# The last two row tiles of an output projection taken together, state sums spread between products, and one subtraction moved ahead of the weight sums

## The chip, the cores and the metric

The kernel runs on one core of a Trainium2 chip. The metric is the device time of one execution in microseconds. For the kernel before it is 1906.66 us, the median of three runs (1905.7 to 1906.89).

## What is computed

One decoder block on 2048 positions of 1024 channels, in float32:

```python
h = rmsnorm(x, norm_mix); proj = h @ w_in
c = conv4(proj[:, :512]); y_lru = rg_lru(c) * gelu(proj[:, 512:1024])
glu = proj[:, 1024:1536] * sigmoid(proj[:, 1536:])
y_cm = silu(layernorm(conv31(glu)))
x = x + concat(rmsnorm(y_lru), rmsnorm(y_cm)) @ w_out
h = rmsnorm(x, norm_ffn)
x = x + (silu(h @ w_gate) * (h @ w_up)) @ w_down
return rmsnorm(x, norm_final)
```

## The kernel before, in words

Every float32 product is made of three float32r products, high by high, high by low and low by high: an operand's high part is a rounding copy (by ScalarE as a rule), its low part is a subtraction (by GpSimd or VectorE). Four things follow one another: the input projection with both branches (to about 415 us), the output projection (415 to 624 us), the gate and up projections by a Strassen-like scheme of seven products (to about 1470 us for both halves of the positions), and the down projection.

**Output projection.** The 2048 positions are 16 row tiles, NT = 16, here called rows 0 to 15. A row has four products of 12 matmuls, one for each bank e = 0 to 3: e 0 and 1 (group 0) take the first four channel chunks (the LRU branch), e 2 and 3 (group 1) the last four. VectorE adds each bank, scaled, to the residual line (add_row, line 1729), counting s_outf[e]; TensorE's product for bank e of row w waits until the same bank of row w - 1 has been read. ScalarE splits y into y_hi (y_split, line 1260), GpSimd makes y_lo (line 888). After add_row, ScalarE takes the root of the row's mean square (row_std, lines 1351 and 1352), VectorE scales the row (row_scaled, hn, line 1903), TensorE transposes it (turn_h2, line 2312) after the next row's products, and ScalarE copies the transposed tile out (h2_copy, line 1346).

Beside rows 1 to 9 the normalisation of the two branches runs. Its sums over channels are matmuls with a vector of 1/512: norm_columns (line 2195) has one output column per matmul. For m = 1 it has no folded operand, so it makes 16 such sums, recorded as 32 matmuls, after row 1; norm_var (line 2187) comes right behind it.

**Into the gate and up projections.** For the first half the seven moving operands a[0] to a[6] are made while the last rows run: VectorE sums four of them (first_half_sum), ScalarE makes the high parts (a_high, line 1356), and GpSimd makes the low parts 0, 1 and 6 (a_low, line 938), VectorE 2, 3, 4 and 5 (a_low, line 1863). VectorE also makes the weight sums of every matrix, four instructions (weight_sum, line 1887); ScalarE and GpSimd split them (t_hi, line 1366, t_lo, line 933), and the raw weights (b_hi, b_lo, line 927). t_sum, a_hi[2] and a_hi[3] lie where the group 0 weights of the output projection were, a_hi[4] to a_hi[6] where those of group 1 were, so the first can begin when the last product of group 0 is done.

Matrix m has products n = 0 to 6, each 12 matmuls, in the order 0 (matrix m), then 1, 2, 3, 4, 5, then 0 of the next matrix, then 6. Product n of the first matrix of a half waits for low part n. Before products 4 and 5 of the first matrix TensorE also turns rows 14 and 15.

Each engine runs its instructions in the order written. The order on GpSimd at rows 14 and 15 is: y_lo of row 14, b_lo, a_lo 0, y_lo of row 15, a_lo 1. On VectorE, with row 15: bank reads of group 0, four weight sums, a_lo 2, bank reads of group 1, a_lo 3; then in the first matrix_block a sum, hn of row 14, a_lo 4, hn of row 15, a_lo 5, four weight sums of the next matrix.

The second half starts in second_half_block (VectorE): a sum of product results, a_lo 4 and 5, the four weight sums, sum12, a_lo 6, sum22. Product 6 of that matrix waits for sum22 (gt, line 1959).

Of the kernel before, what the change touches and what calls it, by code (L numbers as in the profile page):

```python
# [22 lines left out]
P = 128  # L23
TILE = 512
# [6 lines left out]
def hybrid_block(nc, x, norm_mix, w_in, conv4_w, conv4_b, gate_a_w, gate_a_b, gate_x_w, gate_x_b,  # L31
# [4 lines left out]
    NJ = CH // P  # L36
# [7 lines left out]
    NT = S // P  # L44
# [32 lines left out]
    with ExitStack() as ctx:  # L77
# [332 lines left out]
        def yb(w):  # L410

            return 4 + w if w < 2 else (w + 1) % 2 if w < TPH else 2 + w % 2

        def from_sbuf(w):

# [371 lines left out]
        def _(pool):  # L787
# [164 lines left out]
            for w in range(3, NT):  # L952
                if w > 4:
                    y_lo_part(w)
                if w == NT - 2:
                    raw_lo(0, 0)
                    pool.wait_ge(s_sum0, 4)
                    a_low(0)
                if w == NT - 1:
                    a_low(1)  # L960
                for m, first in NORM_STEP.items():
                    if w == {2: 3, 3: 6}[m]:
                        fold(m, "mean")
                    if w - first == 2:
                        for what in ("lru", "var") if m == 2 else ("var", "lru"):
                            fold(m, what)
                    if w - first == 4:
                        fold(m, "cm")
# [89 lines left out]
        def _(act):  # L1058
# [313 lines left out]
            for w in range(NT):  # L1372
                if w == 1:
                    row_std(1)
                    norm_swish(1, between=DIRECT[1], turned=0)
                    h2_copy(1)
                if 4 <= w < NT - 1:
                    y_split(w + 1)
                if w == 4:
                    norm_rms_cm(1, 5)  # L1380
                for m, first in NORM_STEP.items():
                    if w - first == 1:
                        squares_lru(m)
                        if w == 4:
                            h2_copy(2)
                            h2_copy(3)
                        squares_cm(m)
                    if w - first == 2:
                        norm_std(m, 5)
                        if m == 2:  # L1390
                            norm_rms_lru(m, 4)
                    if w - first == 3:
                        norm_swish(m)
                    if w - first == 4:
                        norm_rms_cm(m, 5)
                if w == NT - 1:
                    act.wait_ge(s_sum0, 4)
                    act.wait_ge(s_out[1], NT)
                    a_high(2)
                    sums_hi(0, 0)  # L1400
                    a_high(3)
                    row_std(w)
                if 5 <= w < NT - 1:
                    h2_copy(w - 1)
                if 1 < w < NT - 1:
                    row_std(w)
                if w - NORM_STEP[3] == 3:
                    norm_rms_lru(3, 4)
                if w == LOAD_AT + 3:
                    act.wait_ge(s_a0, 64)  # L1410
                    a_high(0)
                    a_high(1)
                    raw_hi(0, 0, 1)
# [154 lines left out]
        def _(dve):  # L1568
# [143 lines left out]
            def add_row(w, between=None, groups=(0, 1)):  # L1712

                if w == 4:
                    norm_rms(1)
                if w % 4 == 0:
                    dve.wait_ge(s_rms, w // 4 + 1)
                dve.wait_ge(s_xr[w % 4], 16 * (w // 4 + 1 + (2, 1, 1, 1)[w % 4]))
                line = row[w % 4]
                for group in groups:  # L1720
                    if group and between:
                        between()
                    for dh in range(2):
                        e = 2 * group + dh
                        cols = slice(dh * TILE, (dh + 1) * TILE)
                        dve.wait_ge(s_out[e], w + 1)
                        if group:
                            dve.wait_ge(s_outf[dh], w + 1)
                        v.scalar_tensor_tensor(out=line[:, cols], in0=ps[e],
                                               scalar=rms[:, 2 * w + group:2 * w + group + 1],  # L1730
                                               in1=line[:, cols], op0=ALU.mult, op1=ALU.add).then_inc(s_outf[e], 1)

# [156 lines left out]
            def first_weight_sums():  # L1889
                for n in range(4):  # L1890
                    weight_sum(0, 0, n, 1)
                a_low(0, 2)

            def row_scaled(w):
                dve.wait_ge(s_std2, w + 1)
# [17 lines left out]
            for w in range(NT):  # L1913
                if w == 0:
                    add_row(2)
                    row_scaled(0)
                elif w > 2:
                    add_row(w, first_weight_sums if w == NT - 1 else lambda: norm_between(w))
                if w == NT - 1:
                    a_low(0, 3)  # L1920
                if w == 3:
                    row_scaled(2)
                if w == 1 or 3 <= w < NT - 2:
                    row_scaled(w)
                for m, first in NORM_STEP.items():
                    if w - first == 4:
                        norm_rms(m)
                if w in SUM_AT:
                    for n in range(2):
                        first_half_sum(2 * SUM_AT.index(w) + n)  # L1930
# [62 lines left out]
            def matrix_block(m, i, b, h, first=False, count=None, last=False, early=(), late=(), second=False):  # L1993

                if first and not b:
# [1 line left out]
                    row_scaled(NT - 2)  # L1997
                    a_low(0, early[0])
                    row_scaled(NT - 1)
                    a_low(0, early[1])  # L2000
                    dve.wait_ge(s_hn, NT)
                    for n in range(2):
                        dve.wait_ge(s_x2st[n], 16 * NT // 2)
# [26 lines left out]
            def second_half_block(m, i, count):  # L2030

                sum11(m, i, 0, 1, True)
                a_low(1, 4)
                a_low(1, 5)
                dve.wait_ge(s_pr[6], m)
                for n in range(4):
                    weight_sum(m + 1, 1, n, count)
                sum12(m, i, 0, 1, True)
                a_low(1, 6)
                sum22(m, i, 0, 1, True)  # L2040
                hidden21(i - 1, 0)
                for n in range(2):
# [2 lines left out]
                f_sum(2, i - 1, 0)  # L2045
                f_sum2(i - 1, 0)

            matrix_block(0, 0, 0, 0, first=True, count=1, early=(4, 5))
            matrix_block(1, 0, 1, 0, first=True, count=2)
            for h in range(NH):  # L2050
                if h:
# [74 lines left out]
        def _(pe):  # L2126
# [60 lines left out]
                    mm = pe.matmul(ps[bank], mean_w[:, :], tile[:, j], start=j == 0, stop=j == chunks - 1)  # L2187
                mm.then_inc(done, 1)

            def norm_columns(m, what, bank, done):  # L2190

                tile, chunks = summed(m, what)
                for t in range(TILE // P):
                    for j in range(chunks):
                        mm = pe.matmul(ps[bank][:, t:t + 1], tile[:, j, t * P:(t + 1) * P], mean_w[:, 0:1],
                                       start=j == 0, stop=j == chunks - 1)
                mm.then_inc(done, 1)

            def norm_mean(m, bank):
                norm_rows(m, "mean", bank, s_mean)  # L2200
# [1 line left out]
            def norm_var(m, bank):  # L2202
                norm_rows(m, "var", bank, s_var)

            def norm_sums_lru(m, bank):
                norm_columns(m, "lru", bank, s_rm2)

            def norm_sums_cm(m, bank):
                norm_columns(m, "cm", bank, s_rm1)
# [131 lines left out]
                        pe.wait_ge(s_dc, m + 1)  # L2341
                        norm_sums_lru(m, 4)

            for w in range(NT):
                b = yb(w)
                pe.wait_ge(s_ylo, w + 1)
                for group in range(2):
                    if group:
                        norm_sums(w)
                    if w == 0:  # L2350
                        pe.wait_ge(s_wlo, FIRST_APART + PPAIRS + WOQ // 2 * (group + 1))
                    for dh in range(2):
                        e = 2 * group + dh
                        if e == 3:
                            norm_steps(w)
                        cols = slice(dh * TILE, (dh + 1) * TILE)
                        if w:
                            pe.wait_ge(s_outf[e], w)
                        elif e == 3:
                            gates_tile(UNITS - 1, 1)  # L2360
                            pe.wait_ge(s_dc, 2)
                        product(ps[e],
                                (lambda k: y_hi[b][:, k], lambda k: y_lo[b][:, k]),
                                (lambda k: wo_hi[:, k, cols], lambda k: wo_lo[:, k, cols]),
                                range(group * NJ, (group + 1) * NJ)).then_inc(s_out[e], 1)
                if w == 1:
                    free_aux(1, AUX_USES)
                    norm_sums_lru(1, 7)
                    free_aux(0, AUX_USES)
                    norm_var(1, 6)  # L2370
                for turned in TURNED.get(w, (w - 1,) if 5 <= w < NT - 1 else ()):
                    turn_h2(turned)


            BANKS = [[ps[4], ps[5], ps[0], ps[5], ps[0], ps[5], ps[5]], [ps[4], ps[1], ps[0], ps[1], ps[0], ps[1], ps[1]]]
# [42 lines left out]
            def last_rows(n):  # L2418

                if n in (4, 5):  # L2420
                    turn_h2(NT - 6 + n)
                if n == 2:
                    for e in range(2):
                        pe.wait_ge(s_outf[e], NT)

            pe.wait_ge(s_rsty, 4)
            pe.wait_ge(s_rsts, 4)
            matrix_product(0, 0, 0, 0, 0, first=True)
            two_matrices(0, 0, new_half=0, first=True, between=last_rows)
            for h in range(NH):  # L2430
# [64 lines left out]
```

## Time and profile before

| | |
|---|---|
| median of three runs | 1906.66 us (1905.7 to 1906.89) |
| the profiled execution | 1904.58 us |
| its span in the profile | 1902.7 us |
| TensorE busy | 1875.1 us, 99% of the span |
| VectorE, ScalarE, GpSimd busy | 1106.6, 808.4, 1144.9 us |
| mean granted TensorE clock | 0.996 |

A granted clock of 1.00 is 2.4 GHz, 0.50 is 1.2 GHz. Times of the trace count from the start of the span. Matmuls are pipelined: the start of the next tells more than the length of one. PE is TensorE, DVE is VectorE, ACT is ScalarE, POOL is GpSimd. In a row of the timeline the first number is the start, the second the length from first to last of the merged instructions, both in us.

### The profile page before, as it was taken

Reading aid. Unit: us, or ns where it says so; the run is one execution under the profiler, and the core shown is the slowest. Engines: PE = TensorE matmul, PEld = TensorE weight load, DVE = VectorE, ACT = ScalarE, POOL = GpSimd, SP = SyncE. Lnnn points to the kernel's source line nnn. Section 1 sums busy time; section 2 is a strip of 40 time slices with the busy share of each in tenths; the row PEclk is TensorE's granted clock in tenths of the full one; section 3 lists DMA queues with packets and bytes.
Section 4 is the critical chain, followed back from the end, with each engine's and each line's share of the span. In section 5 each row is a group of like instructions: output and inputs, shape, how many; then the busy total and the mean of one; then the engine's idle time right before and its main releaser. Section 6 shows DMA issues by size and latency. Waiting matters only on the chain.

```text
span 1902.7 us, 22499 instructions
## 1 busy us (share of the span) xinstructions
PE 1875.1 (99%) x8374; PEld 1544.2 (81%) x8374; DVE 1106.6 (58%) x1269; ACT 808.4 (42%) x938; POOL 1144.9 (60%) x427
## 2 busy tenths in 40 slices
PE   9999999999999999999999999999999999999998
PEld 7888788877788788888888788888888888888886
DVE  6899988997645755455545854445443025433535
ACT  6466766585643533333333433333333222232235
POOL 3577477945734465666655755555555676676663
PEclk9999999999999999999999999999999999999999
DMA  6222132265777334533355433323333765655455
GB/s 196 78 79 88 45 100 78 75 224 172 247 240 231 117 125 127 153 119 127 112 153 176 151 105 114 106 88 105 115 105 127 288 225 190 210 189 211 166 198 221
DMA packets 240946, 284.20 MB, mean 149 GB/s; under 512 B 12095, under 2 KB 166207, under 8 KB 240364
## 3 DMA queue, kind: packets, MB, share of 16 engines
q1 hardware_dynamic: 240874, 283.25, 44.8%
q8 instruction: 45, 0.74, 0.2%
q14 instruction: 25, 0.20, 0.0%
q10 hardware_dynamic: 2, 0.00, 0.0%
HBM read 200.90 MB, written 82.31 MB: 149 GB/s over the span
## 4 chain that ended last, share of the span: by engine, by line
PE 82%; POOL 6%; DVE 5%; ACT 2%; issue 2%; DMA 2%; POOLq 0%; SPq 0%; DVEq 0%; ACTq 0%
PE ps L2133 19%; PE ps L2135 19%; PE ps L2134 19%; PE acc L2133 8%; PE acc L2135 8%; PE acc L2134 8%; DVE a_lo L1863 1%; POOL nsq L877 1%; PE ps L2161 1%; DVE t_sum L1887 1%; POOL nsq L879 1%; POOL w_lo L804 1%; POOL f_lo L1018 0%; DVE wo_lo L1707 0%; POOL glu L827 0%
## 5 line engine op out<-in xcount | busy, mean ns | idle before, releaser
L933 POOL TENSOR_TENSOR t_lo<-t_sum,t_hi 128x2048 fp32r<-128x2048 f32 x44 | 205.6, 4674 | 165.3 <-ACT t_hi L1366 165.2
L927 POOL TENSOR_TENSOR b_lo<-m_raw,b_hi 128x1536 fp32r<-128x1536 f32 x44 | 157.6, 3582 | 179.2 <-ACT b_hi L1361 121.9
L1018 POOL TENSOR_TENSOR f_lo<-f_raw,f_hi 128x2048 fp32r<-128x2048 f32 (+1 forms) x42 | 182.2, 4338 | 129.3 <-ACT f_hi L1518 124.8
L2133 PE MATMUL ps<-h_hi,w_hi 128*128 128x512 f32 x512 | 201.1, 393 | 0.8 <-POOL w_lo L804 0.8
L2135 PE MATMUL ps<-h_hi,w_lo 128*128 128x512 f32 x512 | 199.4, 389 | 0.0
L2134 PE MATMUL ps<-h_lo,w_hi 128*128 128x512 f32 x512 | 199.2, 389 | 0.0
L1887 DVE TENSOR_TENSOR t_sum<-m_raw 128x512 f32<-128x512 f32 x88 | 141.7, 1630 | 97.4 <-PE acc L2135 87.6
L1518 ACT CAST f_hi<-f_raw 128x2048 fp32r<-128x2048 f32 (+1 forms) x42 | 74.3, 1769 | 263.6 <-PE ps L2135 168.1
L2133 PE MATMUL ps<-wd_hi,f_hi 128*128 128x512 f32 x462 | 179.8, 389 | 0.8 <-POOL wd_lo L1025 0.8
L2134 PE MATMUL ps<-wd_lo,f_hi 128*128 128x512 f32 x462 | 179.7, 389 | 0.0
L2135 PE MATMUL ps<-wd_hi,f_lo 128*128 128x512 f32 x462 | 179.7, 389 | 0.0
L2076 DVE TENSOR_TENSOR wd_raw<-wd_raw 128x1024 f32<-128x1024 f32 (+1 forms) x30 | 73.6, 2453 | 174.8 <-DMA wd_raw<-in_w_down 174.8
L2133 PE MATMUL ps<-a_hi,t_hi 128*128 128x512 f32 x440 | 171.5, 390 | 0.8 <-DVE p5s L1959 0.8
L2134 PE MATMUL ps<-a_lo,t_hi 128*128 128x512 f32 x440 | 171.2, 389 | 0.0
L2135 PE MATMUL ps<-a_hi,t_lo 128*128 128x512 f32 x440 | 171.2, 389 | 0.0
L2133 PEld LDWEIGHTS ps<-h_hi,w_hi 128*128 128x128 f32 x512 | 96.1, 188 | 20.8 <-POOL w_lo L804 1.2
L2135 PEld LDWEIGHTS ps<-h_hi,w_lo 128*128 128x128 f32 x512 | 96.1, 188 | 20.3
L2134 PEld LDWEIGHTS ps<-h_lo,w_hi 128*128 128x128 f32 x512 | 96.2, 188 | 19.6 <-issue 0.2
L2133 PE MATMUL acc<-a_hi,t_hi 128*128 128x512 f32 x264 | 103.7, 393 | 4.0 <-DVE gt L1959 2.4
L2133 PE MATMUL ps<-a_hi,b_hi 128*128 128x512 f32 x264 | 102.9, 390 | 4.2 <-DVE a_lo L1863 2.6
L2133 PE MATMUL ps<-wo_hi,y_hi 128*128 128x512 f32 x256 | 104.6, 409 | 2.3 <-DVE wo_lo L1707 1.0
L2134 PE MATMUL acc<-a_lo,t_hi 128*128 128x512 f32 x264 | 103.3, 391 | 0.0
(257 smaller groups left out, 4689.1 us busy)
## 6 DMA issues: line engine op xcount, KB each, us to landing
f_raw<-f_scr SPq DMA_DIRECT2D x35, 1024.0 KB, 4.9
wd_raw<-in_w_down SPq DMA_DIRECT2D x60, 512.0 KB, 6.6
f_scr<-fs SPq DMA_DIRECT2D x110, 256.0 KB, 2.1
m_raw<-in_w_gate SPq DMA_DIRECT2D x88, 256.0 KB, 3.9
m_raw<-in_w_up SPq DMA_DIRECT2D x88, 256.0 KB, 5.1
w_raw<-in_w_in SPq DMA_DIRECT2D x32, 512.0 KB, 5.3
f_scr<-gt SPq DMA_DIRECT2D x44, 256.0 KB, 2.0
xt<-in_x SPq DMA_DIRECT2D x16, 512.0 KB, 6.3
```

The costliest lines, as they stand in the source:

```text
L804: g.tensor_tensor(w_lo[q % 2][:, :, :, :], w_raw[q % 2][:, :, :, :], f32(w_hi[q % 2][:, :, :, :]), ALU.subtract).then_inc(s_wlo, 1)
L877: g.tensor_tensor(into[:, 0:2], source[:, 0:2], source[:, 2:4], ALU.add).then_inc(s_fold, 1)
L879: g.tensor_tensor(into[:, 0], into[:, 0], into[:, 1], ALU.add).then_inc(s_fold, 1)
L927: g.tensor_tensor(b_lo[b][:, :, :, :], m_raw[b][:, 0:3], f32(b_hi[b][:, :, :, :]), ALU.subtract).then_inc(s_mlo, 1)
L933: g.tensor_tensor(t_lo[b][:, :, :, :], t_sum[b][:, :, :, :], f32(t_hi[b][:, :, :, :]), ALU.subtract).then_inc(s_mlo, 1)
L1018: g.tensor_tensor(f_lo[j % 3][:, 0:n], f_raw[j % 2][:, 0:n], f32(f_hi[j % 3][:, 0:n]), ALU.subtract).then_inc(s_dlo, 1)
L1518: a.copy(f_hi[j % 3][:, 0:n], f_raw[j % 2][:, 0:n]).then_inc(s_dhi, 1)
L1887: v.tensor_tensor(into, in0, in1, ALU.subtract).then_inc(s_t, 1)
L2076: v.tensor_tensor(raw[:, 0, 0:c1 - c0], raw[:, 0, 0:c1 - c0], raw[:, 1, 0:c1 - c0], WD[m][2]).then_inc(s_t, 1)
L2133: pe.matmul(bank, lhs[0](c), rhs[0](c), start=first, stop=False, skip_group_check=more)
L2134: pe.matmul(bank, lhs[0](c), rhs[1](c), start=False, stop=False, skip_group_check=more)
L2135: mm = pe.matmul(bank, lhs[1](c), rhs[0](c), start=False, stop=last, skip_group_check=more)
```

## The change

Five edits:

1. The state sums of m = 1 are spread: after each of the four products of row 1, TensorE makes the sums of one of four groups of 128 positions (8 recorded matmuls).
2. Rows 14 and 15 are interleaved on TensorE: group 0 of row 14, group 0 of row 15 (into banks 4 and 5, out_bank), the turning of row 13, group 1 of row 14, group 1 of row 15. VectorE reads in the order row 14 group 0, row 15 group 0, the four weight sums, row 14 group 1, a_lo 2, row 15 group 1, a_lo 3, a_lo 4.
3. To have y of row 15 earlier, ScalarE's y_split(15) goes ahead of row_std(13), and GpSimd makes y_lo of row 15 right after that of row 14; b_lo, a_lo 0 and a_lo 1 follow.
4. ScalarE's a_high(2), sums_hi and a_high(3) move to row 14, around h2_copy(13) and ahead of row_std(14).
5. In the second half's first block VectorE makes a_lo 6 ahead of the weight sums.

```diff
 GpSimd
             for w in range(3, NT):
                 if w > 4:
                     y_lo_part(w)
-                if w == NT - 2:
+                if w == NT - 1:
                     raw_lo(0, 0)
                     pool.wait_ge(s_sum0, 4)
                     a_low(0)
-                if w == NT - 1:
                     a_low(1)
 ScalarE
-                if 4 <= w < NT - 1:
+                if 4 <= w < NT - 2:
                     y_split(w + 1)
...
-                if w == NT - 1:
+                if w == NT - 2:
                     act.wait_ge(s_sum0, 4)
                     act.wait_ge(s_out[1], NT)
                     a_high(2)
+                if 5 <= w < NT - 1:
+                    h2_copy(w - 1)
+                if w == NT - 3:
+                    y_split(NT - 1)
+                if w == NT - 2:
                     sums_hi(0, 0)
                     a_high(3)
-                    row_std(w)
-                if 5 <= w < NT - 1:
-                    h2_copy(w - 1)
-                if 1 < w < NT - 1:
+                if w > 1:
                     row_std(w)
 VectorE
+                elif 2 < w < NT - 2:
+                    add_row(w, lambda: norm_between(w))
+                elif w == NT - 2:
+                    add_row(NT - 2, groups=(0,))
+                    add_row(NT - 1, groups=(0,))
+                    first_weight_sums()
+                    add_row(NT - 2, groups=(1,))
+                    a_low(0, 2)
+                elif w == NT - 1:
+                    add_row(NT - 1, groups=(1,))
                     a_low(0, 3)
+                    a_low(0, 4)
...
                     row_scaled(NT - 2)
                     a_low(0, early[0])
                     row_scaled(NT - 1)
-                    a_low(0, early[1])
...
                 a_low(1, 4)
                 a_low(1, 5)
+                a_low(1, 6)
                 dve.wait_ge(s_pr[6], m)
                 for n in range(4):
                     weight_sum(m + 1, 1, n, count)
                 sum12(m, i, 0, 1, True)
-                a_low(1, 6)
                 sum22(m, i, 0, 1, True)
...
-            matrix_block(0, 0, 0, 0, first=True, count=1, early=(4, 5))
+            matrix_block(0, 0, 0, 0, first=True, count=1, early=(5,))
 TensorE
+        def out_bank(w, e):
+            return 4 + e if w == NT - 1 and e < 2 else e
...
+            def row_group(w, group):
...
+                    if w and out_bank(w, e) == e:
+                        pe.wait_ge(s_outf[e], w)
...
+                    if w == 1:
+                        free_aux(1, AUX_USES)
+                        norm_sums_lru(1, 7, (e,))
+
+            for w in range(NT - 1):
+                row_group(w, 0)
+                if w == NT - 2:
+                    row_group(NT - 1, 0)
+                    turn_h2(w - 1)
+                row_group(w, 1)
...
+            row_group(NT - 1, 1)
```

The wait of the first matrix for the reads of banks 0 and 1 of row 15 moves ahead of its product 0, and the waits for the last normalisation sums move to the start of row 15.

## Rows read from the trace of the kernel before

**Rows 1.** The page, busy time of TensorE over the span.
```profile
PE 1875.1 (99%) x8374; PEld 1544.2 (81%) x8374; DVE 1106.6 (58%) x1269; ACT 808.4 (42%) x938; POOL 1144.9 (60%) x427
```
**Rows 2.** Waits of TensorE, whole run: total us, times, longest.
```profile
PE ps L2133 <- DVE a_lo L1863: 2.6, 1, 2.6
PE acc L2133 <- DVE gt L1959: 2.4, 1, 2.4
...
PE acc L2133 <- POOL a_lo L938: 1.6, 1, 1.6
...
PE ps L2133 <- DVE row L1729: 0.6, 1, 0.6
```
**Rows 3.** Timeline of TensorE between rows 1 and 2.
```profile
439.45 3.94 PE L2195 MATMUL ps<-mean_w,ny 128*128 128x1 f32 x32
443.25 2.05 PE L2187 MATMUL ps<-nsq,mean_w 128*128 128x512 f32 x2
```
**Rows 4.** Windows: stretch, length, TensorE busy (count), granted clock, DMA share, GB/s.
```profile
442.60:449.40 6.80, 6.80 (x18) 0.50 0.11 46
...
638.70:642.20 3.50, 3.50 (x19) 1.00 0.31 93
...
1074.10:1077.50 3.40, 3.40 (x10) 0.50 0.23 67
```
**Rows 5.** Timeline of VectorE and GpSimd during row 2.
```profile
447.99 4.45 DVE L1697 TENSOR_TENSOR_SCAN cv<-uw,hl,su 128x1024 f32<-128x1024 f32 x1 [0.21 <-POOL su L869]
...
457.92 0.75 DVE L1729 SCALAR_TENSOR_TENSOR row<-ps,rms,row 128x512 f32<-128x512 f32 x1
...
447.91 2.39 POOL L888 TENSOR_TENSOR y_lo<-y_raw,y_hi 128x1024 fp32r<-128x1024 f32 x1
```
**Rows 6.** Timeline of TensorE: rows 14 and 15 begin, product 6.
```profile
601.34 0.47 PE L2133 MATMUL ps<-wo_hi,y_hi 128*128 128x512 f32 x1
...
613.14 0.48 PE L2133 MATMUL ps<-wo_hi,y_hi 128*128 128x512 f32 x1
...
649.59 0.50 PE L2133 MATMUL acc<-a_hi,t_hi 128*128 128x512 f32 x1 [1.56 <-POOL a_lo L938]
```
**Rows 7.** Timeline of ScalarE, rows 13 and 14.
```profile
601.24 1.07 ACT L1346 COPY h2t<-ps 128x512 f32<-128x512 f32 x2 [2.92 <-PE ps L2312]
...
603.60 1.04 ACT L1260 CAST y_hi<-y_raw 128x1024 fp32r<-128x1024 f32 x1
```
**Rows 8.** Timeline of GpSimd from row 14 to the first matrix.
```profile
600.75 3.50 POOL L927 TENSOR_TENSOR b_lo<-m_raw,b_hi 128x1536 fp32r<-128x1536 f32 x1
...
612.12 4.61 POOL L938 TENSOR_TENSOR a_lo<-a_raw,a_hi 128x2048 fp32r<-128x2048 f32 x1
624.32 4.67 POOL L933 TENSOR_TENSOR t_lo<-t_sum,t_hi 128x2048 fp32r<-128x2048 f32 x1 [7.59 <-ACT t_hi L1366]
```
**Rows 9.** Timeline of VectorE from row 13 to the first matrix.
```profile
603.92 1.42 DVE L1903 SCALAR_TENSOR_TENSOR hn<-row,rstd,g_row 128x1024 f32<-128x1024 f32 x1
...
619.55 1.28 DVE L1887 TENSOR_TENSOR t_sum<-m_raw 128x512 f32<-128x512 f32 x2
...
626.09 5.05 DVE L1863 TENSOR_TENSOR a_lo<-a_raw,a_hi 128x2048 fp32r<-128x2048 f32 x1 [0.28 <-ACT a_hi L1356]
...
633.05 5.57 DVE L1863 TENSOR_TENSOR a_lo<-a_raw,a_hi 128x2048 fp32r<-128x2048 f32 x1
```
**Rows 10.** Timeline of VectorE and GpSimd, start of the second half.
```profile
1057.82 6.07 DVE L1863 TENSOR_TENSOR a_lo<-a_raw,a_hi 128x2048 fp32r<-128x2048 f32 x2
1063.82 4.59 DVE L1887 TENSOR_TENSOR t_sum<-m_raw 128x512 f32<-128x512 f32 x2
...
1061.71 5.55 POOL L927 TENSOR_TENSOR b_lo<-m_raw,b_hi 128x1536 fp32r<-128x1536 f32 x1
```
**Rows 11.** Timeline of ScalarE and VectorE, a[6] of the second half.
```profile
1063.32 1.93 ACT L1356 CAST a_hi<-a_raw 128x2048 fp32r<-128x2048 f32 x1
...
1070.38 2.28 DVE L1863 TENSOR_TENSOR a_lo<-a_raw,a_hi 128x2048 fp32r<-128x2048 f32 x1
```

More of the change, by code:

```diff
@@ L1728, in add_row @@
                             dve.wait_ge(s_outf[dh], w + 1)
-                        v.scalar_tensor_tensor(out=line[:, cols], in0=ps[e],
+                        v.scalar_tensor_tensor(out=line[:, cols], in0=ps[out_bank(w, e)],
                                                scalar=rms[:, 2 * w + group:2 * w + group + 1],
@@ L1891, in first_weight_sums @@
                     weight_sum(0, 0, n, 1)
-                a_low(0, 2)
             def row_scaled(w):
@@ L1916, in _ @@
                     row_scaled(0)
-                elif w > 2:
-                    add_row(w, first_weight_sums if w == NT - 1 else lambda: norm_between(w))
-                if w == NT - 1:
+                elif 2 < w < NT - 2:
[8 more added lines that the diff above has]
+                    add_row(NT - 1, groups=(1,))
                     a_low(0, 3)
+                    a_low(0, 4)
                 if w == 3:
@@ L2188, in norm_rows, with norm_columns @@
                 mm.then_inc(done, 1)
-            def norm_columns(m, what, bank, done):
+            def norm_columns(m, what, bank, done, tiles=range(TILE // P)):
                 tile, chunks = summed(m, what)
-                for t in range(TILE // P):
+                for t in tiles:
                     for j in range(chunks):
@@ L2196, in norm_columns @@
                                        start=j == 0, stop=j == chunks - 1)
-                mm.then_inc(done, 1)
+                if t == TILE // P - 1:
+                    mm.then_inc(done, 1)
             def norm_mean(m, bank):
@@ L2203, in norm_var, with norm_sums_lru @@
                 norm_rows(m, "var", bank, s_var)
-            def norm_sums_lru(m, bank):
-                norm_columns(m, "lru", bank, s_rm2)
+            def norm_sums_lru(m, bank, tiles=range(TILE // P)):
+                norm_columns(m, "lru", bank, s_rm2, tiles)
             def norm_sums_cm(m, bank):
@@ L2342, in norm_steps @@
                         norm_sums_lru(m, 4)
-            for w in range(NT):
+            def row_group(w, group):
                 b = yb(w)
[L2346 to L2365, printed above, removed]
+                if not group:
+                    pe.wait_ge(s_ylo, w + 1)
+                    if w == NT - 1:
+                        pe.wait_ge(s_rsty, 4)
+                        pe.wait_ge(s_rsts, 4)
+                else:
+                    norm_sums(w)
+                if w == 0:
+                    pe.wait_ge(s_wlo, FIRST_APART + PPAIRS + WOQ // 2 * (group + 1))
+                for dh in range(2):
+                    e = 2 * group + dh
+                    if e == 3:
+                        norm_steps(w)
+                    cols = slice(dh * TILE, (dh + 1) * TILE)
+                    if w and out_bank(w, e) == e:
+                        pe.wait_ge(s_outf[e], w)
+                    elif e == 3:
+                        gates_tile(UNITS - 1, 1)
+                        pe.wait_ge(s_dc, 2)
+                    product(ps[out_bank(w, e)],
+                            (lambda k: y_hi[b][:, k], lambda k: y_lo[b][:, k]),
+                            (lambda k: wo_hi[:, k, cols], lambda k: wo_lo[:, k, cols]),
+                            range(group * NJ, (group + 1) * NJ)).then_inc(s_out[e], 1)
+                    if w == 1:
+                        free_aux(1, AUX_USES)
+                        norm_sums_lru(1, 7, (e,))
@@ L2366, in _ @@
+            for w in range(NT - 1):
[4 more added lines that the diff above has]
+                row_group(w, 1)
                 if w == 1:
-                    free_aux(1, AUX_USES)
-                    norm_sums_lru(1, 7)
                     free_aux(0, AUX_USES)
                     norm_var(1, 6)
-                for turned in TURNED.get(w, (w - 1,) if 5 <= w < NT - 1 else ()):
+                for turned in TURNED.get(w, (w - 1,) if 5 <= w < NT - 2 else ()):
@@ L2421, in last_rows @@
                     turn_h2(NT - 6 + n)
[L2422 to L2427, printed above, removed]
+            for e in range(2):
+                pe.wait_ge(s_outf[e], NT)
             matrix_product(0, 0, 0, 0, 0, first=True)
```

## The prediction

> **What bounds the kernel now.** I read the page first: TensorE is busy for 1875.1 of 1902.7 us [rows 1], so only its idle time and its slow clock can be won, and only where the change touches them. The waits of TensorE come next [rows 2]: in the first matrix of the first half it waits 2.6 us for a low part by VectorE (operand 4) and 1.6 us for one by GpSimd (operand 6), in the first block of the second half 2.4 us for VectorE's sum22, and ahead of row 3 it waits 0.6 us for VectorE's read of row 2. These are the four places that the edits reach. Third, the granted clock [rows 4]: it is 0.50 (1.2 GHz) for the 6.8 us from 442.6, behind the thin sums of row 1, and for the 3.4 us from 1074.1, behind the 2.4 us wait; behind the 2.6 us wait in the first half it stays at 1.00. Last, the timelines around each place, engine by engine [rows 3, 5 to 11].
>
> A product of twelve matmuls takes 2.72 us: row 15 begins 11.80 us after row 14 [rows 6], which holds 48 matmuls and a turning of 0.9 us, so 0.227 us a matmul. At the half clock it is about 0.43 us: ten matmuls touch the 3.40 us from 1074.1 [rows 4], of which the first and the last reach over its ends, so some 8 fit where 15 would.
>
> **State sums spread (edit 1).** Thirty-two thin matmuls take 3.94 us behind row 1 and norm_var starts at 443.25 [rows 3]. Spread, they take as long, 8 behind each product, so norm_var starts when it did. What should go is the half clock of [rows 4]: 13 or so products of row 2 and norm_var ran in it, and row 2 should end some 3 us earlier, near 455.0 instead of 458.0 (48 matmuls of 0.227 us from about 444.1). But row 3 then waits for VectorE's read of row 2's bank 0. It starts at 457.92 and lasts 0.75 [rows 5], and nothing in front of it depends on TensorE's rows: the scan takes 4.45 us from 447.99, since GpSimd's y_lo of 447.91 to 450.30 goes first [rows 5], then come a reciprocal and a scaling. Bank 3 of row 1 is finished 1.3 us later than VectorE asks for it (the sums of three products stand ahead of it, 2.7 us), so VectorE's convolution ends 1.3 us later; the scan would be issued at 449.3 and still get through behind the same y_lo at 450.3, so this costs nothing while that cover of 2.3 us holds. The gain is therefore 0, and TensorE's idle time ahead of row 3 grows from 0.6 to about 3.8 us. The half clock followed an idle 2.4 us and not one of 2.6 us, so behind 3.8 us I take it as likely. A stretch of 3.4 us at 0.50 loses 1.6 us (7 matmuls of 0.227 that no longer fit). Bounds: 0 and +3.2 (6.8 us of it, as in the first case); I take +1.6, from the 3.4 us case, which also followed an idle wait.
>
> **Rows 14 and 15 (edits 2 to 4).** TensorE's work is the same and it is full up to 618.7, if y_lo of row 15 is there at 606.8 (601.3 + 5.45). ScalarE makes y_hi of row 15 right behind the copy of row 12, which ends at 602.3 [rows 7], so 602.2 to 603.3; GpSimd's y_lo takes 2.4 us [rows 5], so 603.4 to 605.8. It is in time by 1 us. For this ScalarE's row_std of row 13 comes 1.04 us later, and VectorE's hn of row 13 is ready to start at 604.96 instead of 603.92 [rows 9].
>
> Now the edit's price. VectorE's two-source operations on SBUF and GpSimd's operations exclude one another, and when both wait they take turns: in [rows 10] b_lo, 3.50 us alone [rows 8], is issued at 1061.71 and takes 5.55, since it waits for VectorE's a_lo to end at 1063.9; the weight sums queued right behind that a_lo don't go first but wait until b_lo has ended at 1067.26 (two sums take 4.59 us instead of 1.28 [rows 9, 10]). Bank reads (0.75 us [rows 5]) have a PSUM source, and I take them as not held. The Trainium skill has the same in "SBUF — State Buffer", in its section on the shared port pair: an exclusive lock, held for the whole instruction by whoever starts first. It names no turn-taking; by its rule alone VectorE could run its four sums in one go, the second rival below.
>
> In order, on GpSimd: y_lo to 605.8; hn of row 13, waiting, goes next (1.15 us), to 606.95; b_lo 3.5 us to 610.4; a_lo 0, 4.6 us [rows 8], to 615.0; then a_lo 1 is queued. VectorE reads bank 1 of row 15 (product ends at 612.4, row 14 and 15 group 0 having taken 10.9 us from 601.3) by 613.3 and asks for the lock with the first weight sum at 613.2. It gets it at 615.0 and ends at 615.6; a_lo 1 takes it to 620.2; the other three sums run to 622.2. The cover that the old order had is gone: a_lo 1 ran 612.12 to 616.7 [rows 8] and the sums began at 619.55 [rows 9]. Queued behind the sums are the reads of row 14 group 1. Bank 2 is read by 622.95, though its product ended at 615.8, and TensorE's product for bank 2 of row 15, due at 618.7, waits for that read: a new stall of 4.3 us. Between bounds of 0 (sums not held) and 6.4 us (a full a_lo 0 or a_lo 1 of 4.6 us plus the 1.8 us) I take 4.3, which is worked out from the rows.
>
> Row 15 then ends at 628.6 instead of 624.1, its last bank is read by 629.4 instead of 625.8. Behind it runs VectorE's chain up to low part 6: in the old order it lost 2.8 us to the lock in one a_lo (5.05 against 2.28) and 3.3 in another (5.57) [rows 9, 11]. In the new one a_lo 3 waits only until t_lo, issued at 624.3 and held to 625.8 by a_lo 2, ends at 630.4 (1.1 us lost), a_lo 4 comes right behind it at 632.9 once ScalarE has its high part, hn of row 14 follows, and a_lo 5 now meets b_lo and loses the 3.5 us in the other's place, which holds hn of row 15 back too. So 1.5 of the 3.6 us come back: the weight sums of the next matrix end near 647.0 and a_lo 6 at 651.7 (4.6 us), product 6 starts at 651.7 instead of 649.59 [rows 6]. The waits of 2.6 and 1.6 us at products 4 and 6 do nearly vanish; the stall at row 15 has taken their place, and 2.1 us more. If the clock falls behind the 4.3 us of idle time (longer than the one that was followed by it), 1.6 to 1.7 us are added, because TensorE is then what product 6 waits for. I take +3.8, with 2.1 without the clock.
>
> ScalarE's moved a_high(2), sums_hi and a_high(3) stand ahead of row_std(14), which costs 1 to 2 us of a slack that hn of row 14 has (it waits for VectorE). SP's stores wait for reads 0 to 3 us later and are not waited for. The moved waits ahead of row 15 and product 0 are long met. All these cost 0; without the cover of hn the row_std order would cost its 1.4 us.
>
> **Second half (edit 5).** Behind a_lo 5 (ends 1063.9) the first sum waits for b_lo until 1067.26 [rows 10]. In the new order a_lo 6 stands there. Its high part is ready at 1065.25 [rows 11], b_lo has the lock by then, and a_lo 6 runs from 1067.3 to 1069.5; four sums, 2.7 us, and sum12 bring sum22 to 1073.4 instead of 1073.26. The same instructions behind the same wait: +0.1, between 0 and +0.6 (what of the first sum lay beside the wait). The sums themselves end 2.3 us later, t_hi and t_lo with them, about 1079, and are needed by 1080.5: 1.5 us of cover is left, and SP's load behind them is for a block later. The stall and the half clock behind it [rows 2, 4] stay.
>
> **Sum.** 1.6 + 3.8 + 0.1 = +5.5 us on the profiled 1904.58 us (1902.7 of span and 1.9 around it), which lies 2.1 us under the median. On the median: 1906.66 + 5.5 = 1912.2 us. About 0.2% (3.8 us) is what a measurement of this kernel can tell from no change.
>
> The Trainium skill's "TensorE: Matmul & The Clock Gate", Part 1, says that the throttled clock is the default and that activity lifts it. By it both longer idles are against the change and the spreading of the sums is for it; the rows show both, and that the gain of the latter is covered by VectorE.
>
> **Rivals.** (a) The collision comes, the clock falls at one of the two places or at neither: 2.2 to 3.9 us more, 1908.9 to 1910.6. For it: a 2.6 us idle left the clock alone. (b) VectorE runs the sums in one go from 615.0, to 617.7. Then bank 2 is read at 618.4 and TensorE does not stall; a_lo 2 waits for a_lo 1 to 622.3, the later low parts meet t_lo and b_lo as before, and product 6 starts about 0.7 us later than before. With edit 1's clock +2.4 us, 1909.1; without, 1907.5. Against it: [rows 10]. (c) Faster: the lock doesn't bind here at all (VectorE's sums 613.3 to 616.0, each low part ahead of its product). Then TensorE waits at 4 no more, and product 6 follows product 0 of the next matrix at 646.9, -2.7 us. If in the second half a_lo 6 gets in ahead of b_lo as well, up to 2.4 us and the 1.7 us of the half clock behind it go too: -6.8, 1899.9. It decides at whether the first sum is issued after a_lo 1 has ended; by the sum above it is 7 us too early. (d) The change does not act: y_lo of row 15 late at 606.8 would merely add its own wait; with 1 us of margin this is the least.
>
> **How the numbers follow.** The forecast with both clock falls 0.38; (a) 0.22; (b) 0.17; (c) 0.18; (d) 0.05. Slower by over 0.2%: the forecast and a part of (a), 0.47. Faster by over 0.2%: most of (c), 0.15. Within: 0.38. Range 1904.0 to 1914.5: down to (c) with the first gain alone, up to the 6.4 us stall bound.
>
> **What would show it.** Right: the weight sums (L1887) in the window 612 to 624 take some 9 us from first to last with a POOL a_lo of 4.6 us between them; a new wait of TensorE on DVE row (L1729) of 3 to 5 us near 619; a wait ahead of row 3 of 3 to 4 us; the clock at 1.00 from 440 to 455 and at 0.50 behind one of the new waits; the waits for a_lo at products 4 and 6 under 1 us; the wait for sum22 unchanged. Wrong: sums of 0.7 us each back to back at 613, or row 3 starting before 457.

## The result and the profile after

The changed kernel takes 1913.17 us, the median of seven runs (1911.92 to 1914.82), against 1906.66 us for the kernel before in seven runs beside it (1904.56 to 1907.8). The ratio is 1.0039, with a 95% interval of 1.0030 to 1.0048: slower by more than 0.2%, 6.5 us on the medians where 5.5 were forecast. The profiled execution took 1913.17 us with a span of 1911.3, which is 8.6 us over the span of before (1902.7).

TensorE's waits of the whole run answer to [rows 2] (us in total, times, longest):

```profile
PE ps L2143 <- DVE row L1733: 7.3, 2, 3.7
PE ps L2143 <- DVE y2s L1954: 3.8, 1, 3.8
...
PE acc L2143 <- DVE gt L1970: 2.4, 1, 2.4
...
PE acc L2143 <- ACT u2s L1460: 0.6, 1, 0.6
...
PE ps L2323 <- DVE hn L1906: 0.6, 1, 0.6
```

The waits of 2.6 us for a_lo 4 and 1.6 us for a_lo 6 are gone. Two waits for a bank read have come, 3.7 us ahead of row 3 and 3.6 us at bank 2 of row 15, and a third, 3.8 us, for VectorE's sum11 (y2s), which the prediction did not have. The wait for sum22 (gt) stays at 2.4 us.

The windows answer to [rows 4]: busy stretches, three idle ones and what follows each of them (length, TensorE busy and count, granted clock, DMA share, GB/s).

```profile
440.00:454.00 14.00, 14.00 (x66) 1.00 0.10 38
454.40:458.20 3.80, 0.13 (x1) 1.00 0.37 143
458.40:461.70 3.30, 3.30 (x9) 0.50 0.88 331
619.80:623.50 3.70, 0.11 (x1) 0.82 0.00 0
623.60:629.00 5.40, 5.40 (x13) 0.50 0.00 0
1078.00:1086.40 8.40, 8.40 (x36) 1.00 0.59 183
1086.50:1090.30 3.80, 0.08 (x1) 0.94 0.42 155
1090.40:1093.20 2.80, 2.80 (x7) 0.50 0.29 106
```

With the sums spread, the clock holds through row 2, which ends at 454.4 instead of 458.0; all of it is then waited away. All three idle stretches of nearly 4 us are followed by 0.50.

VectorE between rows 13 and 15 of the changed kernel (start, length, then the instruction), which answers to [rows 9]:

```profile
605.93 1.96 DVE L1906 SCALAR_TENSOR_TENSOR hn<-row,rstd,g_row 128x1024 f32<-128x1024 f32 x1
...
614.26 7.11 DVE L1891 TENSOR_TENSOR t_sum<-m_raw 128x512 f32<-128x512 f32 x2
621.40 1.42 DVE L1891 TENSOR_TENSOR t_sum<-m_raw,t_sum 128x512 f32<-128x512 f32 x2
622.74 1.40 DVE L1733 SCALAR_TENSOR_TENSOR row<-ps,rms,row 128x512 f32<-128x512 f32 x2
```

and GpSimd beside it, which answers to [rows 8]:

```profile
604.40 2.40 POOL L891 TENSOR_TENSOR y_lo<-y_raw,y_hi 128x1024 fp32r<-128x1024 f32 x1 [2.54 <-ACT y_hi L1262]
606.77 4.48 POOL L930 TENSOR_TENSOR b_lo<-m_raw,b_hi 128x1536 fp32r<-128x1536 f32 x1
611.22 9.61 POOL L941 TENSOR_TENSOR a_lo<-a_raw,a_hi 128x2048 fp32r<-128x2048 f32 x2
```

The first two weight sums take 7.11 us instead of 1.28: they start beside a_lo 0, get one turn when it ends, and wait a whole a_lo 1 for the next. The four sums last from 614.3 to 622.8, and the reads of row 14 stand behind them.

The third stall lies where the second half begins. VectorE:

```profile
1069.80 4.14 DVE L1867 TENSOR_TENSOR a_lo<-a_raw,a_hi 128x2048 fp32r<-128x2048 f32 x1 [1.37 <-ACT a_hi L1358]
...
1078.30 5.72 DVE L1995 TENSOR_TENSOR fs<-gt 128x512 f32<-128x512 f32 x2
1083.94 3.97 DVE L1986 TENSOR_TENSOR fs<-gt 128x512 f32<-128x512 f32 x1
...
1089.64 0.68 DVE L1954 TENSOR_TENSOR y2s<-y2s,ps 128x512 f32<-128x512 f32 x1
```

and GpSimd:

```profile
1078.61 4.86 POOL L936 TENSOR_TENSOR t_lo<-t_sum,t_hi 128x2048 fp32r<-128x2048 f32 x1 [6.82 <-ACT t_hi L1368]
1083.43 3.94 POOL L930 TENSOR_TENSOR b_lo<-m_raw,b_hi 128x1536 fp32r<-128x1536 f32 x1
```

VectorE has five f sums (fs<-gt, 0.68 us each alone) to do ahead of sum11. They take turns with t_lo and, straight behind it, with b_lo: the second sum takes 5.12 us (inside the 5.72 of the first row) and the third 3.97, so sum11 (y2s) comes at 1089.64. TensorE's product 3 needs it and was free at 1086.4.

Where the 8.6 us of span come from can be read off the starts of the same products. Row 3 starts 0.6 us earlier than before (458.25 against 458.81), but this execution was ahead by as much already (GpSimd's y_lo of [rows 5] starts at 447.29 against 447.91). The turning of row 12 comes 1.1 us later (row 3 ran in part at the half clock); product 6 of the first matrix 4.8 us later (654.43 against 649.59); product 6 of the second half's first matrix 4.5 us later; product 1 behind it only 2.9, since before ran there at the half clock and this execution did not; product 3 of that matrix 7.1 and product 4 8.6 us later. From there on the two run in step.

### The profile page after: what moved, and what is told of

The parts are those of the page before. It is cut to its first block, busy times and chain, and to the rows that moved or that the text cites. A ratio compares the mean times of both kernels' runs of the same rounds, so it can differ in the third digit from the quotient of the medians.

```text
span 1911.3 us, 22501 instructions
## 1 busy us (share of the span) xinstructions
PE 1876.7 (98%) x8374; PEld 1544.7 (81%) x8374; DVE 1108.8 (58%) x1269; ACT 807.9 (42%) x938; POOL 1147.1 (60%) x427
## 4 chain that ended last, share of the span: by engine, by line
PE 61%; POOL 2%; issue 2%; DVE 1%; ACT 1%; DMA 0%; POOLq 0%; SPq 0%; DVEq 0%; ACTq 0%
PE ps L2143 13%; PE ps L2145 13%; PE ps L2144 13%; PE acc L2143 7%; PE acc L2144 7%; PE acc L2145 7%; POOL gt L978 0%; POOL f_lo L1020 0%; DMA wd_raw<-in_w_down 0%; DVE t_sum L1891 0%; POOL t_lo L936 0%; POOL a_lo L941 0%; DVE hn L1906 0%; POOL b_lo L930 0%; DVE fs L1986 0%
```

## Experiments

Each kernel was timed beside runs of the kernel before on the same chip, in three groups. The medians of before were 1905.38 us in the first group (27 runs), 1906.36 in the second and 1906.81 in the third (33 each). A ratio is always taken against the runs of before in the same group, and its 95% interval stands in brackets.

**Edit 1 alone.**

```diff
                         product(ps[e], ...).then_inc(s_out[e], 1)
+                        if w == 1:
+                            free_aux(1, AUX_USES)
+                            norm_sums_lru(1, 7, (e,))
```

> Kernel before with edit 1 alone. Theory: the half clock behind row 1 goes, row 2 ends some 3 us earlier, but row 3 still starts near 458 us, when VectorE has read row 2, so TensorE waits 3 to 4 us there and then runs some 1 to 1.6 us at the half clock: +0 to +1.6 us on before. Rival: what row 2 gains reaches the end, -2 to -3 us.

1906.87 us, ratio 1.0007 (0.9998 to 1.0016), or +1.3 us. The windows of its profile show the wait ahead of row 3 and the clock behind it:

```profile
454.00:457.90 3.90, 0.29 (x2) 1.00 0.34 137
458.30:461.70 3.40, 3.40 (x10) 0.50 0.96 367
```

The rival's gain of 2 to 3 us lies outside the interval. Between 0 and the +1.6 of the forecast the interval does not decide.

**Edit 5 alone.**

```diff
                 a_low(1, 4)
                 a_low(1, 5)
+                a_low(1, 6)
...
                 sum12(m, i, 0, 1, True)
-                a_low(1, 6)
```

> Kernel before with edit 5 alone. Theory formed from the changed kernel's trace: the wait for sum22 stays at 2.4 us, and product 3 of the next matrix gets a new wait of 3.5 to 4 us for VectorE's sum11, since t_lo and b_lo on GpSimd now stand back to back beside VectorE's five f sums and take turns with them: +3 to +4.5 us on before. Rival (the prediction's term): +0.1 us, the new wait there comes from the later start of the half and not from this edit.

1909.47 us, ratio 1.0021 (1.0012 to 1.0031), or +4.0 us. Its waits have the third stall, and the 2.4 us for sum22 are still there:

```profile
PE ps L2133 <- DVE row L1729: 3.9, 1, 3.9
PE ps L2133 <- DVE y2s L1943: 3.8, 1, 3.8
```

So this edit, priced at +0.1 us, costs 4 us. The first line is a surprise of another kind: with the sums of row 1 not spread, this execution nevertheless held its clock through row 2 and waited 3.9 us ahead of row 3. What before does there differs between executions.

**Edits 2 to 4 alone** (the changed kernel with edits 1 and 5 undone, the two diffs above reversed).

> Kernel before with edits 2 to 4 alone. Theory: new wait of 3.5 to 4.3 us ahead of bank 2 of row 15, 3.4 to 6.8 us of half clock behind it, the 2.6 and 1.6 us waits at products 4 and 6 under 1 us each: +2.1 us where the clock holds, +3.8 where it falls. Rival: the shift is taken up by the waits behind it, 0 us or less.

1912.02 us, ratio 1.0032 (1.0020 to 1.0044), or +6.1 us. The wait at row 15 is there (3.6 us) and 6.8 us of half clock from 623.5, 1.7 us before that wait ends. The waits for a_lo 4 and a_lo 6 are gone, and two of 0.6 us (for hn of row 14 and for ScalarE's u2s) have come, as in the changed kernel. The interval's lower end is the forecast's +3.8.

**Edits 2 to 4 with a_lo 1 behind the weight sums.**

```diff
                     a_low(0)
+                    pool.wait_ge(s_t, 4)
                     a_low(1)
```

> Edits 2 to 4, and GpSimd waits for the four weight sums before it makes a_lo 1. Theory (turn-taking between GpSimd's a_lo 1 and VectorE's sums makes the stall): the four sums run in one go and end near 618.5, TensorE waits under 1 us at row 15, no half clock there, and the total is 0 to +1.5 us on before. Rival (the sums are late for another reason, or the order of the rows itself costs the time): the wait at row 15 stays at 3 us or more and the total stays at +3 us or more.

1904.79 us, ratio 0.9997 (0.9988 to 1.0006). One added wait on GpSimd takes away the whole cost of the rows. VectorE:

```profile
612.46 2.72 DVE L1892 TENSOR_TENSOR t_sum<-m_raw 128x512 f32<-128x512 f32 x2
615.22 1.42 DVE L1892 TENSOR_TENSOR t_sum<-m_raw,t_sum 128x512 f32<-128x512 f32 x2
616.55 0.74 DVE L1734 SCALAR_TENSOR_TENSOR row<-ps,rms,row 128x512 f32<-128x512 f32 x1
```

and GpSimd:

```profile
609.41 4.62 POOL L941 TENSOR_TENSOR a_lo<-a_raw,a_hi 128x2048 fp32r<-128x2048 f32 x1
616.71 4.64 POOL L941 TENSOR_TENSOR a_lo<-a_raw,a_hi 128x2048 fp32r<-128x2048 f32 x1 [2.68 <-DVE t_sum L1892]
```

The first sum still waits 1.4 us for a_lo 0, the other three run through, the read of bank 2 is done at 617.3, and TensorE has no wait at row 15. Its waits in the first matrix are now three of 1.4 us (for VectorE's sum11), 1.1 us (for hn of row 14) and 1.5 us (for ScalarE's u2s) in place of 2.6 and 1.6; product 6 begins 48.4 us after row 14 begins, in before 48.3. So the early group 0 gains nothing by itself. A likely reason, which no run isolates, is that GpSimd's turns still hold VectorE back: in this profile a_lo 2 takes 4.68 us, a_lo 3 and 4 together 7.60 and hn of row 14 4.12, where one a_lo takes 2.28 and hn 1.28 when nothing holds them.

**Edit 5 with the f sums behind sum11.**

```diff
 second_half_block
-                for n in range(2):
-                    f_sum(n, i - 1, 0)
-                f_sum6(i - 1, 0)
-                f_sum(2, i - 1, 0)
-                f_sum2(i - 1, 0)
 matrix_block of the next matrix
                     sum11(m, i, b, h, first)
+                    if behind:
+                        for n in range(2):
+                            f_sum(n, i - 1, 0)
...
```

> Edit 5, and VectorE's five f sums go behind sum11 of the next matrix. Theory (the f sums taking turns with t_lo and b_lo are what makes sum11 late): the wait of product 3 for sum11 goes from 3.8 us to under 0.5 us, and the total falls from about +4 us to between 0 and +1.5 us on before, part of it perhaps a wait for t_lo at product 2. Rival (a_lo 6 ahead of the weight sums delays t_lo and this alone makes the stall): 3 us or more of wait remain at product 2 or 3.

1904.94 us, ratio 0.9995 (0.9986 to 1.0004): the +4.0 us are gone, and with them the wait at product 3. What makes sum11 late is the f sums ahead of it, not the later t_lo. A wait of 0.9 us for a later sum11 is new. The kernel with the f sums moved and without edit 5, below, has the ratio 0.9996: once they are out of the way, edit 5 costs nothing that can be measured.

**Work without use in an idle wait.** Nine matmuls ahead of product 6 of the second half's first matrix, into a bank that nothing reads.

```diff
+                    if filler and b == 0:
+                        for _ in range(filler):
+                            pe.matmul(ps[6], b_hi[0][:, 2, 0], a_hi[0][:, 0], start=True, stop=True)
                     matrix_product(6, m + b, i, b, ...)
```

> Kernel before, with nine matmuls without use ahead of product 6 of the second half's first matrix, where TensorE otherwise waits 2.4 us. They write a bank that nothing reads. Theory (the idle wait is what the half clock follows): the 3.4 us at 0.50 near 1074 go, product 6 starts when it did, -1.6 us on before. Rival: the half clock comes all the same or product 6 starts later, 0 us or more.

1908.2 us, ratio 1.0009 (1.0000 to 1.0018): the forecast of -1.6 us was wrong. The windows show why: the clock holds behind the filled wait (0.4 us of it is left, and product 6 starts 0.83 us after sum22 starts, as in before), and 8 us later there is another wait, 2.8 us for sum11, with 6.8 us of half clock behind it.

```profile
1072.60:1080.70 8.10, 8.04 (x36) 1.00 0.44 144
1080.90:1083.80 2.90, 0.18 (x1) 0.90 0.34 126
1083.90:1090.00 6.10, 6.10 (x14) 0.50 0.18 66
```

GpSimd in the same run:

```profile
1071.14 5.24 POOL L933 TENSOR_TENSOR t_lo<-t_sum,t_hi 128x2048 fp32r<-128x2048 f32 x1 [4.62 <-ACT t_hi L1366]
1077.73 3.75 POOL L927 TENSOR_TENSOR b_lo<-m_raw,b_hi 128x1536 fp32r<-128x1536 f32 x1 [1.35 <-ACT b_hi L1361]
```

and VectorE:

```profile
1077.45 0.68 DVE L1975 TENSOR_TENSOR fs<-gt 128x512 f32<-128x512 f32 x1
1078.06 3.97 DVE L1984 TENSOR_TENSOR fs<-gt 128x512 f32<-128x512 f32 x1
```

A faster product 6 lets ScalarE make b_hi earlier, so b_lo comes at 1077.73 instead of 1080.06 and finds the f sums not yet done: one of them waits 3.3 us, and sum11 with it. In before the half clock hides this collision by keeping TensorE back. Profiles of kernels that were not edited here bear this out. Where the clock held behind the 2.4 us wait (edit 1 alone, and edit 1 with a filler below) product 3 waits the same 2.8 us; where it fell at once (before, and edits 2 to 4 with a_lo 1 late) it does not wait; and where it fell 1.2 us after the start of product 6 (edits 2 to 4 alone) it waits 1.1 us.

**Edit 1 with fourteen such matmuls ahead of row 3.**

```diff
+                if w == 3:
+                    pe.wait_ge(s_nstd, 2)
+                    pe.wait_ge(s_rsty, 2)
+                    for _ in range(14):
+                        pe.matmul(ps[6], wo_hi[:, 0, 0:P], wo_hi[:, 0, 0:TILE], start=True, stop=True)
```

> Edit 1, with fourteen matmuls without use ahead of row 3, where TensorE otherwise waits 3.7 us. Theory: the clock stays at 1.00 from 420 us to row 4, row 3 starts when it did, -1.6 us on edit 1 alone, so -0.8 to 0 us on before (before has the cheap half clock behind row 1 in some executions and the dear one at row 3 in others). Rival: the half clock does not depend on the wait, no change on edit 1 alone (+1.3 us on before).

1906.15 us, ratio 0.9996 (0.9987 to 1.0005). Row 3 starts with a wait of 0.5 us and the clock is at 1.00 from 413 to 637 us, where the wait for a_lo 4 has the half clock behind it. Against edit 1 alone (1.0007) it fits the -1.6 us, but the two intervals overlap and the time of the filler alone is not shown.

**Both fillers, the rows with a_lo 1 late, spread sums, edit 5 undone** (the diffs above, put together).

> Changed kernel with edit 5 undone, GpSimd's a_lo 1 behind the weight sums, and both fillers (ahead of row 3 and of product 6 of the second half). Theory: the terms add: 0 for the rows, 0 for the spread sums with the clock held, -1.6 for the filler in the second half and some -1 for the one at row 3: -2 to -3 us on before. Rival: the held clock is given back in longer waits, 0 us.

1906.55 us, ratio 1.0002 (0.9993 to 1.0011): the expected -2 to -3 us did not come. The clock holds from 412 us to 1084, and there the wait of 2.8 us at product 3 appears, as with the single filler.

**The f sums moved, as in the diff above, and nothing else.**

> Kernel before, with only VectorE's five f sums of the second half's first block moved behind sum11 of the next matrix. Theory: before itself loses time there in those executions in which the clock holds at 1074 (b_lo is then ready early and takes a turn between the f sums, 2.8 us of wait at product 3); without it -1 to -2 us on before. Rival: before has this stall in no execution that matters, 0 us.

1905.07 us, ratio 0.9996 (0.9987 to 1.0005), -0.8 us (-2.5 to +1.0). In its profile the clock holds behind the 2.4 us wait and product 3 does not wait, as the theory says; but the interval holds both the theory's time and its rival's, so it is open what before loses there by itself.

**The changed kernel with both collisions taken away**, all five edits kept: the wait ahead of a_lo 1 and the f sums' move, as in the diffs above.

> Changed kernel with the two collisions taken away: a_lo 1 of GpSimd behind the weight sums, f sums behind sum11; all five edits stay. Theory: the two terms of about +3.2 promille and +2.1 promille both go, what is left is edit 1's: 0 to +1.5 us on before. Rival (something else in the change costs too): +3 us or more.

1905.87 us, ratio 0.9998 (0.9989 to 1.0007). A wait on GpSimd and a move in VectorE's order turn +0.39% into no difference. Whatever else the change costs or gains lies within the interval, 2.1 us down and 1.3 us up.

**All that helps together:** rows with a_lo 1 late, spread sums, both fillers, f sums behind sum11; once with edit 5 undone and once with it.

> Rows together with a_lo 1 late, spread sums, both fillers, edit 5 undone, f sums behind sum11. Theory: the filler's gain at 1074 is no longer given back at product 3, the clock holds from 412 us to the end: -3 to -4 us on before. Rival: given back in a later wait, 0 to -1 us.

> The same with edit 5 kept. Theory: a wait of about 1 us for sum11 of a later matrix as in edit 5 with late f sums, else the same: -2 to -4 us on before. Rival: edit 5 costs 2 us or more even so.

Without edit 5: 1902.88 us, ratio 0.9984 (0.9975 to 0.9993), or -3.1 us where -3 to -4 were expected. With it: 1903.69 us, 0.9988 (0.9979 to 0.9997), or -2.3 us where -2 to -4 were expected. These two are the only kernels of the study whose intervals lie below 1. They don't differ from one another beyond their intervals, so edit 5 neither gains nor costs here. Windows of before, over the places of its half clock:

```profile
440.00:462.00 22.00, 21.37 (x92) 0.84 0.27 96
1070.00:1095.00 25.00, 22.60 (x93) 0.93 0.32 106
```

and the same of the kernel without edit 5:

```profile
440.00:462.00 22.00, 21.55 (x97) 1.00 0.27 102
1070.00:1095.00 25.00, 24.60 (x109) 1.00 0.31 105
```

Every window of 50 us from 412 to 1862 us reads 1.00 in that profile, product 3 does not wait, and the kernel's 11 runs lie within 1.8 us (1901.95 to 1903.75) where the 33 of before beside it spread over 6.7. The same kernel without the f sums' move gained nothing (1.0002), and the f sums' move alone gave 0.9996, so by the medians the gain needs the move and something of the rest together; the intervals of these kernels still touch or overlap a little. Which of the two fillers brings it was not separated.

## Why the prediction was right, and where it was not

**Rows 14 and 15: right, in its mechanism and place.** The step put y_lo of row 15 at 603.4 to 605.8, the first sum's turn at 615.0, a_lo 1 to 620.2, the sums' end at 622.2, the read of bank 2 at 622.95 and product 6 at 651.7 without the clock. Measured, with this execution some 1.1 us late by then: 604.4 to 606.8, 615.8, 620.8, 622.8, 623.5 and 654.43. The added wait that undoes the collision undoes the cost, which shows the cause. The idle wait was 3.6 us and not 4.3, and the half clock lasted 6.8 us (5.4 of them on matmuls) and not the 3.4 that the step assumed. One detail went to the wrong instruction: b_lo held up hn of row 15 (4.33 us instead of 1.28) and not a_lo 5 (2.28). The size was somewhat off: +3.8 forecast, +3.8 between the turning of row 12 and product 6 in the profile, +6.1 us (3.8 to 8.4) in the runs of these edits alone.

The step also took from before that a wait of 2.6 us leaves the clock alone. That was one execution's luck: of the six profiles in which TensorE waits 2.6 us for a_lo 4, four have 3.4 us of half clock right behind it (edit 1 alone, edit 1 with the filler, edit 5 with the f sums late, the f sums' move alone) and two have not (before, edit 5 alone).

**Spread sums: right.** The half clock of [rows 4] went, row 2 ended 3.6 us earlier (3.0 without the 0.6 by which this execution was ahead), VectorE's read came when it did (457.4 against 457.9, again the 0.6), and the idle wait of 3.7 us was followed by 3.4 us at 0.50. Forecast +1.6, measured +1.3 (-0.4 to +3.0). What the step did not know is that before itself does one or the other. Of seven profiles without edit 1 three have the 6.8 us of half clock behind row 1 and a short wait at row 3, two have a wait of 3.9 us there with the half clock behind it, and two have something between (3.4 us of half clock behind row 1 and a wait of 2.3 us). With edit 1 and no filler all three profiles have the dear form. The measured interval holds 0 as well, so that the edit costs anything is not shown.

**Second half: wrong.** The failed step is "+0.1, between 0 and +0.6" for edit 5; it measured +4.0 us (2.3 to 5.9). Its first part held: a_lo 6 waits for b_lo in the first sum's place and sum22 is not late. What failed was "needed by 1080.5: 1.5 us of cover is left". It costed the delay of t_lo only by who reads t_lo, and not by whom t_lo holds up. VectorE's five f sums stand beside it, and the later t_lo reaches up to the next b_lo, so that they now lose two turns, 7.7 us (5.12 and 3.97 for two sums of 0.68), ahead of sum11, where in before they lose one of 3.2 us (4.45 for two). The rule for this was in the prediction, in the step on rows 14 and 15, and was applied there only. Not all of the 3.8 us at product 3 is edit 5's own: kernels without it wait 2.8 us there when the clock holds behind the sum22 wait. That also touches the step's last sentence, "the stall and the half clock behind it stay": the stall stayed, the half clock did not come in this execution, and whether it comes changes from one execution to the next (four profiles of ten).

**The sum.** +5.5 us forecast, +6.5 on the medians and +7.4 (5.7 to 9.2) by the ratio. That the total came out is in part luck: the second half's missing 4 us, and the rows' 2 us more, stand against terms that do not add in full. The three parts alone give 1.3, 6.1 and 4.0, together 11.4, against 7.4 for the whole. Their intervals are some 2 us to either side, so this gap of 4.0 us may be little more than noise; it was not separated further.

**Two sentences of the prediction against the trace.** The Trainium skill's page "SBUF — State Buffer", in its section "SBUF: two separate sides", has an exclusive lock for the whole instruction, and the trace agrees (in the changed kernel the second weight sum, 0.68 us alone, took 5.07 us from 616.30, beside the a_lo 1 that ended at 620.8). With it alone, rival (b), the stall would not have come; the turn-taking of [rows 10] decided. The Trainium skill's page "TensorE: Matmul & The Clock Gate", Part 1, says that activity lifts the throttle, which the fillers show: in four profiles with the filler ahead of row 3 the clock held there, in three with edit 1 and without it, it fell.

## What to carry to other kernels

Two engines that exclude one another also took turns here when both had work queued: a run of short instructions (0.68 us each) can lose one long one of the other engine (3.5 or 4.6 us) between every two of them. When work is moved, look for what then runs beside it on the other engine, not only for who reads its result; and put a wait in front of the long instruction where nobody needs it yet. A stall or a slow clock can keep an engine back just enough to hide a collision behind it, so a gain there may be given back at once, until the order behind it is mended too. And one profile shows one execution: what the clock does behind a short wait has to be looked up in several before a forecast leans on it.

## What the runs showed of the hardware

- The wait of 2.4 us for sum22 was followed by 3.4 us at the half clock in four profiles of ten that had it and the same work around it (before, edits 2 to 4 alone, these with a_lo 1 late, the changed kernel mended), and left the clock alone in the other six. The wait of 2.6 us for a_lo 4 was followed by it in four profiles of six, the wait of 2.8 us for sum11 in all four that had it, and the nine waits of 3.6 to 3.9 us all were. What decides in the cases that go both ways is open.
- Thirty-two matmuls with one output column, 3.94 us in all [rows 3], were followed by 6.8 us of half clock in three profiles of seven and by 3.4 us in two more, though TensorE counts as busy throughout; with 8 of them behind each product it did not come in any of the seven profiles that have edit 1.
- Matmuls without use in a bank that nothing reads held the clock at the place in all the profiles that have them (four ahead of row 3, four ahead of product 6), and where they fit into the wait they delayed nothing: product 6 started 0.83 us after VectorE's sum22 did, with nine of them (1071.83 to 1072.66) as without (1072.58 to 1073.41).
- VectorE's reads of a PSUM bank were not held by GpSimd: in before one took 0.73 us at 605.26 beside GpSimd's a_lo of 604.21 to 609.8, and with a_lo 1 late one took 0.75 us at 618.15 beside the a_lo of 616.71 to 621.35. Elsewhere a read takes 0.75 us too.
